# Splitting the later weight tiles of a hybrid decoder layer ahead of and behind the dilated heads' value groups

## The reference

```python
h = layer_norm(x, ln0_g, ln0_b)
proj = jnp.einsum('btd,dc->btc', h, w_in[l])
qa, ka, va, qb, kb, vb, gate = jnp.split(proj, split_at, axis=-1)
ya = dilated_mixture(heads_a(qa), heads_a(ka), heads_a(va), rel_bias)
yb = stick_breaking(heads_b(qb), heads_b(kb), heads_b(vb))
y = jnp.concatenate([ya, yb], axis=-1) * jax.nn.silu(gate)
out = jnp.einsum('btc,cd->btd', y, w_out[l]) + b_out[l]
h = layer_norm(DEEPNORM_ALPHA * h + out, ln_g[l], ln_b[l])
```

## Time and profile before

| | |
|---|---|
| median of 3 runs | 1777.67 us |
| lowest and highest run | 1776.24 and 1787.24 us |
| the profiled execution's own time | 1777.95 us |
| span of its trace | 1776.0 us |
| PE busy, share of the span | 1658.8 us, 93% |
| DVE busy | 1172.9 us, 66% |
| ACT busy | 797.8 us, 45% |
| mean granted clock of PE | 0.97 |

### The profile page before, as it was taken

One profiled execution on the slowest core, in us unless ns is written; L12 is line 12 of the kernel. 1 busy time (PEld: TensorE's weight loads), 2 busy tenths in 40 slices (PEclk: granted clock), 3 DMA queues, 4 the chain that ended last, 5 costly groups with the idle time before them and its releaser, 6 DMA issues. The chain is left out here.

```text
span 1776.0 us, 27634 instructions
## 1 busy us (share of the span) xinstructions
PE 1658.8 (93%) x9138; PEld 1405.7 (79%) x9138; DVE 1172.9 (66%) x2323; ACT 797.8 (45%) x1993; POOL 331.0 (19%) x207
## 2 busy tenths in 40 slices
PE   5789999998897999999999999998999899949998
PEld 4577888877786888888878787887999899937886
DVE  5531123322224888888888888886888787865996
ACT  3341112211212555555555555555898787931000
POOL 2102100000000000000000000000487677500331
PEclk9899999999998999999999999998999998969999
DMA  4316964599728564845575556433677777456541
GB/s 157 151 49 218 329 225 166 200 307 322 250 107 250 182 188 142 275 139 176 172 236 171 170 155 211 151 113 105 196 204 222 219 227 213 133 162 213 181 142 59
DMA packets 222069, 332.48 MB, mean 187 GB/s; under 512 B 52269, under 2 KB 145896, under 8 KB 215596
## 3 DMA queue, kind: packets, MB, share of 16 engines
q1 hardware_dynamic: 217452, 321.35, 57.2%
q0 software_dynamic: 2400, 9.48, 1.6%
q10 hardware_dynamic: 2080, 0.01, 0.1%
HBM read 204.05 MB, written 122.39 MB: 184 GB/s over the span
## 5 line engine op out<-in xcount | busy, mean ns | idle before, releaser
L1048 ACT ACTIVATE WT_hi<-wt_ps 128x512 fp32r<-128x512 f32 (+1 forms) x320 | 171.1, 535 | 315.9 <-PE wt_ps L980 315.9
L1094 DVE TENSOR_TENSOR_SCAN W<-w,W,zeros 128x512 f32<-128x512 f32 x192 | 248.2, 1293 | 59.2 <-ACT w L1040 58.5
L378 PE MATMUL proj<-h_hi,w_hi 128*128 128x512 f32 x640 | 262.4, 410 | 24.5 <-DVE h_lo L554 16.2
L378 PE MATMUL proj<-h_hi,w_lo 128*128 128x512 f32 x640 | 254.7, 398 | 0.0
L378 PE MATMUL proj<-h_lo,w_hi 128*128 128x512 f32 x640 | 254.5, 398 | 0.0
L1102 DVE TENSOR_TENSOR WT_lo<-wt_ps,WT_hi 128x512 fp32r<-128x512 f32 (+1 forms) x320 | 187.3, 585 | 2.2 <-ACT WT_hi L1048 2.2
L1438 ACT ACTIVATE prob<-neg_s,rows 128x256 f32<-128x256 f32 (+1 forms) x384 | 173.5, 454 | 14.7 <-DVE rows L1498 13.1
L980 PE MATMUL wt_ps<-ident,W 128*128 128x128 f32 x1088 | 173.5, 275 | 6.7 <-DVE WT_lo L1102 5.9
L1040 ACT ACTIVATE w<-z_ps 128x512 f32<-128x512 f32 (+2 forms) x320 | 169.1, 528 | 20.5 <-PE z_ps L970 20.5
L980 PEld LDWEIGHTS wt_ps<-ident,W 128*128 128x128 f32 x1088 | 131.7, 140 | 43.3 <-DVE WT_lo L1102 15.5
L378 PEld LDWEIGHTS proj<-h_hi,w_hi 128*128 128x128 f32 x640 | 123.6, 193 | 52.4 <-DVE h_lo L554 17.9
(11 more groups left out here) (157 smaller groups left out, 3467.3 us busy)
## 6 DMA issues: line engine op xcount, KB each, us to landing
va_d<-st SPq DMA_DIRECT2D x96, 256.0 KB, 4.0
wa_hi<-wa_d SPq DMA_DIRECT2D x48, 512.0 KB, 3.9
wa_lo<-wa_d SPq DMA_DIRECT2D x48, 512.0 KB, 5.1
va<-va_d SPq DMA_DIRECT2D x24, 1024.0 KB, 8.6
wa_d<-x_sb SPq DMA_DIRECT2D x24, 512.0 KB, 4.4
w_raw<-in_w_tiles SPq DMA_DIRECT2D x18, 512.0 KB, 5.2
x_sb<-in_x SPq DMA_DIRECT2D x16, 512.0 KB, 5.7
qk_hi_d<-st SPq DMA_DIRECT2D x32, 256.0 KB, 2.7
```

The source lines that it names most:

```text
L378: last = pe.matmul(acc[n % ACC_SLOTS][:], w[w_slot(t)][:, k, :], h[ch][:, k, :], start=(k, a) == (0, 0), stop=(k, a) == (KD - 1, 2))
L1048: act.activation(WT_hi[n % PART_SLOTS][:, cols], t_ps[n % T_SLOTS][:, cols], ACT.Copy) \
L1094: dve.tensor_tensor_scan(W[n % W_SLOTS][:, 0:width][:, ::-1], w[n % W_IN][:, 0:width][:, ::-1], above[:, ::-1], first, ALU.mult, ALU.max). ...
```

## The change

A list `A_AT` replaces the rule for the places. Later tiles 0 to 5 are split at groups 36, 38, 40, 42, 44 and 46 (all `vb`), tiles 6 to 11 at 66, 68, 70, 72, 74 and 76 (all gate). The load stands 4 groups ahead of the split, the stores one group behind it as before. All instructions are the same ones in the same number; every line of the file below the list moves down by one.

```diff
-    A_FIRST, A_EVERY, A_SLOTS = 40, 3, 4
+    A_AT, A_SLOTS = (36, 38, 40, 42, 44, 46, 66, 68, 70, 72, 74, 76), 4
@@ SyncE
-                a, late = divmod(n - A_FIRST, A_EVERY)
-                if late == 0 and 0 <= a + 2 < A_TILES:
-                    load_wa(a + 2)
-                if late == 1 and 0 <= a < A_TILES:
-                    store_wa(a)
+                for a, place in enumerate(A_AT):
+                    if n == place - 4:
+                        load_wa(a)
+                    if n == place + 1:
+                        store_wa(a)
@@ ScalarE and VectorE, each
-                a, late = divmod(n - A_FIRST, A_EVERY)
-                if late == 0 and 0 <= a < A_TILES:
+                if n in A_AT:
+                    a = A_AT.index(n)
```

## The result

| | before | changed |
|---|---|---|
| median of the first comparison (4 runs each) | 1782.45 us | 1760.85 us |
| median of a second comparison (11 and 6 runs) | 1777.85 us | 1758.83 us |
| the profiled execution's own time | 1777.95 us | 1758.86 us |
| span of its trace | 1776.0 us | 1757.0 us |

The ratio of the first comparison is 0.9888, 95% interval 0.9842 to 0.9934; that of the second 0.9880, 0.9854 to 0.9905. The change makes the kernel 1.2% faster; the forecast was 1760.4 us, a ratio of 0.990. The median of the kernel before stands 4.8 us above the 1777.67 us that the forecast started from, since a fourth run of 1788.09 us came in.

What follows compares the result with a forecast made beforehand. PE was taken to bound the kernel, with late DMA costing 17.8 us in the `va` and first gate groups; 17.8 us given back less 0.5 us kept made 17.3 us, hence 1760.4 us, range 1758.5 to 1769.

Steps and rivals of the forecast that it cites:

- The size of the loss, 17.8 us,: End of group 47 to that of 79: 200.9 us taken against 183.1 from the pace of undisturbed groups.
- The cause: Later tiles' DMAs among the `va` stores: 29.9 us of DMA demand against 23.7 us of PE over four groups.
- The chain through the load of `w_raw`: In `va` and first gate groups: a late `w_raw` load stalls ACT, then DVE, then PE, 12.0 us idle.
- The balance after the change: In the `va` groups without later tiles, DMA demand 23.6 us against 23.7 us of PE over four groups.
- SP's issue time: In the `va` groups SP issues for 4.98 us a group, 20.7 us over four groups of 23.7, so it fits.
- The tight place: `w_raw` load for tile 17, at group 65: 0.5 us lost, with 0 and 5.5 us as ends.
- The slack of the queue, 5 to 7 us,: `va` groups before the change: the queue can run some 5 to 7 us late before PE feels it.
- What it costs where it goes: Later tiles moved to `vb` and gate groups: DMA share about 0.6 to 0.7 in `vb`, no wait, cost nothing.
- The rival that ends slower: `w_raw` loads come late in the `vb` groups, three boundaries costing 23 us in all: 1783 us, chance 0.05.
- The one that the later tiles were not the cause: `va` stores with one raw weight buffer are late anyway, so no gain: 1775 to 1778 us, chance 0.07.
- the rival that the `va` stores alone saturate DMA: `va` groups: arrears grow 0.3 us a tile, 3 to 8 us kept, 1763 to 1768 us, chance 0.24.
- The signs in the profile: Group 47 to 79 in 183 to 185 us, no PE wait over 1 us, clock 1.00, set DMA shares and ACT waits.

Runs made afterwards that it cites:

- all tiles ahead: Changed kernel with all twelve later tiles split ahead of the `va` groups, at groups 31 to 48: 183.8 us from group 47 to 79, ratio 0.9880.
- two tiles back: Changed kernel with two of the six gate splits put back into the `va` groups, at 53 and 59: 190.9 us from group 47 to 79.
- the last kernels: Changed kernel with `w_raw` loads one group earlier, gate splits one group later, or all later tiles ahead of the `va` groups: 183.1, 183.2, 183.8 us.
- the early load in the changed kernel: Changed kernel with each load of `w_raw` one group earlier: 183.1 us from group 47 to 79, ratio 0.9892.
- the later gate splits: Changed kernel with the six gate splits one group later (67, 69, 71, 73, 75, 77): 183.2 us from group 47 to 79.

## Why the prediction was right, point by point

**The size of the loss, 17.8 us,** was read from the pace of whole groups, and this step carries the result: kernels without a wait take 183.1 to 183.5 us for what was put at 183.1.

**The cause** was argued from demand: 29.9 us of DMA in four groups of 23.7. The two experiments that put back only DMAs or only splits show that the DMAs cost the time. Whether the DMA engines or SP's issuing is what runs full is argued from DMA's shares of 0.96 and 1.04, not shown. The chain through the load of `w_raw` was half of the picture: moving the loads earlier gave back only 3.6 us, and the waits passed to the store buffers (29.2 to 61.8 us), which the prediction did not look at.

**The balance after the change,** 23.6 against 23.7 us, held: PE waited for nothing in the `va` groups, with DMA at 94.8% from 349 to 430 us. (What was taken out is 21.9 us and not 23.5: five loads went, but the one at group 62 came in, so four and five pairs of stores are gone.) By the rate that the Trainium skill gives as the HBM limit (DMA: Bandwidth & Descriptors, Specifications, about 358 GB/s) there would have been an estimated microsecond to spare in each group. The trace has 279 and 286 GB/s in two groups with nothing but `va_d` stores, at shares of 0.94 and 0.96, so it speaks against taking that figure for stores of this shape. Nor is it a limit for this kernel elsewhere: with all tiles ahead, DMA moved 414 and 421 GB/s in two slices of 2.2 us in the `vb` groups.

Stretches of the changed kernel, one `va` group each:

```profile
378.70:384.70 6.00, 6.00 (x30) 4.94 (x29) 1.38 (x2) 0.60 (x1) 0.00 (x0) 1.00 0.94 279
...
408.30:414.30 6.00, 6.00 (x30) 4.96 (x29) 1.38 (x2) 0.60 (x1) 0.00 (x0) 1.00 0.96 286
```

**SP's issue time** was put at 4.98 us for a group. It fitted, since SP still waited 17.5 us for finished groups, 12 times, up to 430 us.

**The tight place** was named rightly, group 68 waiting for the split of tile 17, and mis-sized: 0.5 us was taken, 1.1 and 1.3 us were waited, 1.4 and 1.6 us lost. The slack there was 3.6 us less 2 for landing less arrears, so by this sum the arrears were 2.7 us, where the 0.5 us stood for 2.1.

**The slack of the queue, 5 to 7 us,** was the weakest number. With two tiles back, 9.4 us of extra demand, 7.7 us were lost, which leaves 1.7; the 25 us and 17.8 us of before leave 7. A slack of one size can't give both. Proportion can: 3.2 and 3.3 us a tile, 3.6 us with the DMAs alone. Why a tile costs less than the 4.7 us of its DMAs is open. So that "18 to 20 us should be lost" came near 17.8 was in part luck. The forecast did not need it: the 17.8 us were read from the pace.

**What it costs where it goes** was put at nothing: 88.4 us from the end of group 32 to that of group 47 in every trace, also with all twelve tiles ahead. The rival that ends slower fell with that. The one that the later tiles were not the cause fell with their DMAs put back. Of the rival that the `va` stores alone saturate DMA, only its tight place came about.

**The signs in the profile** were mostly met. The stage took 184.5 us (183 to 185 forecast) and the clock was 1.00. Three were missed by a little: PE's wait on `w_lo` was 1.1 us and not under 1, the DMA share of the `vb` groups 0.58 and not 0.6 to 0.7, and the longest wait of ACT for `w_raw` 4.7 us, 5.7 in the second trace, and not 2 to 4.

**The total.** That the forecast of 1760.4 us and the first median of 1760.85 us agree within half a microsecond is in part luck, since the base moved up by 4.8 us. The traces that were compared differ by 19.0 us, of which 16.4 are explained. Over all runs of both comparisons and the one with the last kernels the mean before is 1780.2 us (22 runs), of the changed kernel 1759.9 us (10 runs), 20.2 us apart. The 3.8 us over the 16.4 are not explained. They are about twice what the scatter of the runs leaves uncertain in the difference of the means (each scatters by some 4.5 us). In the second and the last comparison the runs of before have a mean granted clock of 0.968 (18 runs) for 0.975 (6 runs), and the clock behind the waits is in the 16.4 already, so it is likely that before met more of the low clock elsewhere; that this follows from the change was not shown. The stage of the kernel before was traced once, so how much its loss varies from run to run isn't known either. The forecast of 0.97% stood on the phase alone and on the bound of 1%; the measured ratio lies beyond it, in the forecast range all the same.

## What to carry to other kernels

Add up the demand on DMA stage by stage, at the rate that the trace shows for that kind of transfer, and set it against the time that the bounding engine needs for the stage. Here the DMAs of a later tile cost nothing in a stage at 0.47 of DMA's capacity, nor at 0.77, and 3.2 to 3.6 us of their own 4.7 in one that was full, though ACT and DVE had time for the splits. Where one place in a queue is felt first, moving it earlier mostly passed the waits on to the next place (14.2 of 17.8 us stayed lost); moving bytes out of the full stage gave back 16.4. So look at every buffer that waits for the queue, not only at the one with the longest wait. And the ideal time of a stage, from the pace of undisturbed groups, was here a better forecast than the sum of waits (12.0 of the 17.8 us), since it takes in the slow clock behind them.

## What the runs showed of the hardware that was not expected

The total of one run tells little. The kernels with two tiles back, with the early load in the changed kernel and with the later gate splits lost 7 to 14 us against the others behind group 79, where all run the same instructions. The difference stands mainly between 1200 and 1500 us, in the granted clock. This stretch in the changed kernel and in the one with two tiles back:

```profile
1200.00:1500.00 300.00, 281.23 (x2291) 272.56 (x2290) 240.57 (x982) 251.86 (x902) 196.65 (x66) 0.95 0.74 209
```
```profile
1200.00:1500.00 300.00, 284.82 (x2184) 276.25 (x2183) 232.50 (x940) 242.52 (x864) 179.51 (x61) 0.90 0.71 196
```

PE is busy in them for about as long, at a mean of 0.95 against 0.90. The kernel with later gate splits has 0.90 as well, the changed kernel with the early load 0.91, the kernel before 0.95 and the second trace of the changed kernel 0.96. (The counts of matmuls compare less well, as the window does not hold the same work in each.) The waits of PE behind 560 us are alike in all of them, 10.8 to 12.7 us for the costliest kind; what decides how long the clock is low in this stretch, no run here shows. The ten runs of the changed kernel go from 1754.46 to 1770.01 us at mean clocks of 0.977 and 0.966. A difference of a few microseconds between two kernels of this kind is read from the stage, not from the total.
